# New addresses in SBUF for the streamed operands of a float32r transformer kernel's dense matmuls

## What is computed

```python
proj = x @ w_in
return jnp.square(jax.nn.relu(x @ w_up)) @ w_down        # twice
gates = jax.nn.sigmoid(h @ w_gate[l] + b_gate[l])
u = _dwconv_causal(hf @ w_up[l], ffn_dw[l]) + ffn_dw_b[l]
yff = (jax.nn.silu(u_g) * u_v) @ w_down[l]
```

## Time and profile before

| | |
|---|---|
| median of 3 runs | 1269.23 us (1268.73 to 1272.51) |
| profiled execution | 1266.51 us, span of its instructions 1264.5 us |
| granted TensorE clock | 0.998 of 2.4 GHz |
| TensorE matmul busy | 1230.5 us (97%), 10396 instructions |
| TensorE weight load busy | 1191.9 us (94%) |
| VectorE, ScalarE, GpSimd busy | 872.4, 670.5, 58.5 us |
| DMA | 213.11 MB, mean 169 GB/s |

### The profile page before, as it was taken

How to read it: one execution, slowest core, us unless ns; L and a number is a source line. 1 busy time by engine, 2 the same in 40 slices (tenths; PEclk the granted TensorE clock), 3 DMA queues, 4 the chain that set the end, 5 groups by cost and what they waited for, 6 DMA issues and landing times.

```text
span 1264.5 us, 24598 instructions
## 1 busy us (share of the span) xinstructions
PE 1230.5 (97%) x10396; PEld 1191.9 (94%) x10396; DVE 872.4 (69%) x1387; ACT 670.5 (53%) x879; POOL 58.5 (5%) x54
## 2 busy tenths in 40 slices
PE   9989999999998999999999999999999999999998
PEld 8868899999987989999999999999999999999997
DVE  6885865566747687646676434869988667899843
ACT  6454453353456435535435448575455565777741
POOL 0463000000000000000000001000000000000000
PEclk9999999999999999999999999999999999999999
DMA  9222255455349233555542559965445432645430
GB/s 361 97 101 101 100 185 215 166 196 188 131 132 256 102 134 117 217 180 185 192 175 73 200 182 278 284 182 201 157 158 197 167 132 83 218 175 190 167 134 34
DMA packets 30666, 213.11 MB, mean 169 GB/s; under 512 B 3680, under 2 KB 4192, under 8 KB 5232
## 3 DMA queue, kind: packets, MB, share of 16 engines
q1 hardware_dynamic: 27792, 195.83, 42.5%
q0 software_dynamic: 2016, 14.68, 5.8%
q10 hardware_dynamic: 768, 1.31, 0.3%
HBM read 210.76 MB, written 1.05 MB: 168 GB/s over the span
## 4 chain that ended last, share of the span: by engine, by line
PE 57%; DVE 3%; ACT 2%; issue 1%; DVEq 0%; ACTq 0%
PE lin L514 17%; PE lin L515 17%; PE lin L516 16%; ACT whi L1255 1%; PE lin L544 1%; PE lin L551 1%; PE lin L545 1%; PE att L650 1%; PE lin L657 1%; PE lin L694 1%; DVE z L1913 1%; DVE wlo L1803 0%; PE att L730 0%; PE att L769 0%; DVE pr L1944 0%
## 5 line engine op out<-in xcount | busy, mean ns | idle before, releaser
L1803 DVE TENSOR_TENSOR wlo<-raw,whi 128x2048 fp32r<-128x2048 f32 x165 | 377.2, 2290 | 175.4 <-ACT whi L1255 174.4
L514 PE MATMUL lin<-xh,whi 128*128 128x256 f32 x1712 | 481.9, 282 | 1.5 <-POOL wlo L485 1.0
L515 PE MATMUL lin<-xl,whi 128*128 128x256 f32 x1712 | 478.0, 279 | 0.0
L516 PE MATMUL lin<-xh,wlo 128*128 128x256 f32 x1712 | 477.8, 279 | 0.0
L1255 ACT ACTIVATE whi<-raw 128x2048 fp32r<-128x2048 f32 x183 | 348.9, 1908 | 160.5 <-PE lin L516 143.3
L514 PEld LDWEIGHTS lin<-xh,whi 128*128 128x128 f32 x1712 | 321.3, 188 | 4.5 <-issue 2.7
L515 PEld LDWEIGHTS lin<-xl,whi 128*128 128x128 f32 x1712 | 321.2, 188 | 0.6 <-issue 0.5
L516 PEld LDWEIGHTS lin<-xh,wlo 128*128 128x128 f32 x1712 | 321.1, 188 | 0.0
L514 PE MATMUL lin<-fh,whi 128*128 128x256 f32 x512 | 143.8, 281 | 0.0
L516 PE MATMUL lin<-fh,wlo 128*128 128x256 f32 x512 | 143.0, 279 | 0.0
L515 PE MATMUL lin<-fl,whi 128*128 128x256 f32 x512 | 142.8, 279 | 0.0
(11 more groups left out here) (397 smaller groups left out, 1917.0 us busy)
## 6 DMA issues: line engine op xcount, KB each, us to landing
raw<-units_dram SPq DMA_DIRECT2D x183, 1024.0 KB, 4.8
wlo<-units_dram POOLq DMA_DIRECT2D x14, 1024.0 KB, 14.0
h<-x_dram SPq DMA_DIRECT2D x1, 1024.0 KB, 6.9
out_dram<-h SPq DMA_DIRECT2D x4, 256.0 KB, 2.0
consts<-consts_dram SPq DMA_DIRECT2D x1, 864.0 KB, 15.4
narrow_a<-narrow_a_dram SPq DMA_DIRECT2D x1, 544.0 KB, 8.7
aqT<-mem_dram ACTq DMA_DIRECT2D x1, 512.0 KB, 5.7
fkT<-mem_dram ACTq DMA_DIRECT2D x1, 512.0 KB, 6.6
```

The costliest lines, as they stand in the source:

```text
L514: mm(out, w[0], a[0], start=first, stop=False)
L515: mm(out, w[0], a[1], start=False, stop=False)
L516: return mm(out, w[1], a[0], start=False, stop=last)
L1803: v.tensor_tensor(wlo[u % RING][:], raw[u % RING][:], whi[u % RING][:].bitcast(f32), ALU.subtract).then_inc(lo_ready, 1)
```

## The change

Nothing of the program's instructions changes but addresses. The unused tensor ahead of `xh` grows from 16 to 24 words and the one behind `xl` shrinks from 32 to 24, so `xh` and `xl` move by 32 bytes, from 64 to 96 modulo 128, and all behind them stays. In the MLP's group an unused tensor of 24 words is put ahead of `fh` and one of 8 words behind `fl`: `fh` and `fl` move by 96 bytes, from 64 to 32 modulo 128 (of the next line), and `relu` and `sqr` by 128 bytes.

```diff
@@ -229,10 +229,10 @@
         h = sbuf("h", [P, DB, S])
         z = sbuf("z", [P, DB, S])
-        sbuf("ahead_of_x", [P, 16])
+        sbuf("ahead_of_x", [P, 24])
         xh = sbuf("xh", [P, DB, S], f32r)
         xl = sbuf("xl", [P, DB, S], f32r)
-        sbuf("behind_x", [P, 32])
+        sbuf("behind_x", [P, 24])
         consts = sbuf("consts", [P, NC])
@@ -274,8 +274,8 @@
-        fh, fl, relu0, relu1, sqr0, sqr1 = stage(
-            ("fh", [P, 16, S], f32r), ("fl", [P, 16, S], f32r), ("relu0", [P, 2, S]), ("relu1", [P, 2, S]),
+        _, fh, fl, _, relu0, relu1, sqr0, sqr1 = stage(
+            ("ahead_of_f", [P, 24]), ("fh", [P, 16, S], f32r), ("fl", [P, 16, S], f32r), ("behind_f", [P, 8]), ("relu0", [P, 2, S]), ("relu1", [P, 2, S]),
             ("sqr0", [P, 2, S]), ("sqr1", [P, 2, S]))
```

## The result

The changed kernel is slower: a median of 1284.74 us against 1268.98 for the kernel before on the same chips, a ratio of 1.0129 with a 95% interval of 1.0092 to 1.0166. The forecast was 1269, no change. The range held the time, the forecast did not hold the side.

What follows compares the result with a forecast made beforehand. TensorE's stream of dense matmuls was taken as the bound. 1266.5 us profiled, no term, 0 +- 2.6 for redrawn unit starts; with the runs' median 2.7 above the profiled one, forecast 1269, range 1239 to 1303.

Steps and rivals of the forecast that it cites:

- What bounds the kernel: Whole kernel: TensorE busy 97% of the span, a long stream of matmuls; time from one matmul to the next counts.
- The counts (5712, 1536, 432): Touched matmuls: 5712 stream xh or xl, 1536 stream fh or fl, 432 have x as the loaded operand.
- g as the control: Last stage: the 528 matmuls of gh and gl are untouched and must stay at 0.1179 us in every case.
- The sign that I had named for a loss: Feed-forward stage, profile after: 966 or fewer matmuls in 118 us, against 1004 if nothing changes.
- the whole step of 4.5: Dense matmuls: the distance between the two paces found, 0.1178 and 0.1133 us, a step of 0.0045 us each.
- I take zero for the 7248 and 432: All touched matmuls, x and f streamed or x loaded: moving their addresses changes the pace by nothing, 0 us.
- So only the nearest rows: Caveat: the quarter-line pairs that cost nothing are fp32 operands in passes, with another ratio of stream to load.
- clears the home and not the distance: Streams from 0 and 64 share two paces to 0.0002 us, but stream and load are 64 apart both times.
- The closing sentence: Dense matmuls: a surcharge hanging on stream-to-load address distance, which no dense row before varies, would make the prediction wrong.
- The argument that identical addresses give both paces: Dense stream: something other than addresses picks the pace, most simply the stream's start instant against some running clock.
- The straddle rival: Streams from 96 and 32 begin mid 64-byte piece, 17 fetches not 16: +34 us, 1303; slower 0.26 in all.
- The faster rival: Touched units all run at 0.1133 us: -28 us, 1241; without any surcharge 1212; faster 0.30 in all.

## Why the prediction was wrong

**What bounds the kernel** was right: the pace of the dense matmuls goes whole into the time. The counts (5712, 1536, 432) were right, g as the control stayed, and the range held. The sign that I had named for a loss, 966 or fewer matmuls in 118 us, did not come: there were 986, halfway to it from the 1004 of no change, because the loss for x was 2.2 ns in this stage and not the whole step of 4.5. I had priced losses in whole steps only, and the paces after, 0.1200 and 0.1186, lie between none and one.

**The step that failed** is "I take zero for the 7248 and 432". It rested on the earlier trace rows, quarter-line distances that cost nothing. Those pairs keep their distances and their steps in every full kernel (the transposes of pr 108.8 to 108.9 ns, pT against gate 111.6 to 111.7, conv against upad 215.8 to 216.1, h against narrow_a 217.7), so no run shows what another distance would cost them, nor why they pay nothing. They are fp32 operands, and the float32r matmuls, put at quarter-line offsets, did pay. "So only the nearest rows" was the right caution, and I gave it too little weight. In the zero's place the runs show +2.4 ns for x, +0.9 for f and +3.8 for the token units: 16.5 us.

**What I noticed and didn't use.** I wrote that 0 and 64 as homes of the stream had the same paces at a distance of 64 both times, and that this "clears the home and not the distance". It was exactly the distance, and with a period of 256 bytes these are two of them, 64 for x streamed and 192 for the weights streamed, which offer the same two paces. The closing sentence, that a surcharge which hangs on distance would make the prediction wrong, is what happened, but no rival carried it for the worse. The argument that identical addresses give both paces, so something else picks the pace, was half true. The instant of the start picks among the paces that a distance offers (at 64 and 192: 0.1133 or 0.1178), and the distance decides which are on offer (at 96: 0.120 alone).

**The straddle rival** had the right side and a size of +34 us for what became +16. Its mechanism is refuted three times over: x at 32, just as much in the middle of 64 bytes, costs nothing (ratio 0.998), x at 0 costs 1.0%, and x at 96 with weights at 32 costs nothing (ratio 0.9984).

**The faster rival** was wrong for these homes but right that there is room just below: 112 has it, with 7700 matmuls at the pace that I had priced, and -21 us where -28 was the sum for 6950.

**The lot** is larger than the 2.6 us that I allowed. The kernel before ranged from 1263.38 to 1273.95 in 23 runs; a whole stretch of MLP halves can fall to the fast pace, which I had not expected, and the clock's dips add some us: the slower executions have the lower mean clock (1273.95 at 0.989, 1263.73 at 0.997). A single execution can't tell 0.3% from no change here.

On the Trainium skill's two independent read ports ("TensorE: Matmul & The Clock Gate", Step-by-step): the trace disagrees once more, since the pace depends on where the load's address lies from the stream's, so the two reads are not independent here. The prediction also held the dense stream against the 109 ns that it took from Back-to-back issue gap, and called that a disagreement. There the Trainium skill gives the formula for an isolated matmul and not for a stream with a load each, so 113 and 118 ns don't speak against it. The 16-byte lines of the Trainium skill ("SBUF — State Buffer", SBUF cachelines) don't make all multiples of 16 equal here (114.65 to 120.0 ns), but they may show: 112 runs at 115 while 108 and 116, off the line, run at 119.2 to 122.9. Being off the line doesn't cost everywhere, for 100 and 104 run at 119.55 to 120.35, like 96.

What stays open is what is shared by the two reads with a period of 256 bytes, and why the order of the table is not smooth in distance. What the start's instant is measured against wasn't tried either.

## What to carry to other kernels

When a stream of matmuls with a load each is the bound, read its pace from starts or from counts in a stretch, never from busy time, and look for two paces with the same operands: where they exist, placement is worth a table. Such a table costs one run, with streams over a grid of homes behind the end of the real kernel, and the three full kernels forecast from the tables here came out within ranges of 3 to 6 us. Measure the offset between the two operands, modulo 256 bytes and in steps of 16, and don't stop at the multiples that the allocator offers.

## What the runs showed of the hardware

- float32r, 256 columns, a 128 x 128 load each: 0.1133 to 0.123 us a matmul by the homes of the streamed and the loaded operand, at the full clock. With the load at 0, 32, 64 or 96 their offset decides, with a period of 256 bytes; best offset 112, worst tried 116. A load at 16 or 112 gave other paces than its offset has in the table.
- Offset 0, streams and loads equally aligned, is among the slow ones (119.35 to 120.0 ns).
- At some offsets two or three stable paces exist, chosen by when the stream starts (16: 116.65 or 118.75; 192: 113.35 or 117.75; x in the kernel at 64: 113.3 or 117.8). A pace can last for 150 us, across units and from x to f; it changed at some breaks of the stream and at some places where the operands change roles, and not at others. At offset 112 streams go over to 113.3 by themselves.
